# The odd layer's mixer of a decoder step as one program, with three of four channel tiles convolved on TensorE

## What is computed

```python
mod = (silu(c) @ ada_w[l] + ada_b[l])          # 6 x 1024 per layer, one row for each of 9 conditions
sh1, sc1, g1, sh2, sc2, g2 = split(mod, 6)
def odd_mixer(h, w_in, w_out, pool_w, pool_scale, conv_w, conv_b, ln_g, ln_b, pool_hist, conv_hist):
    u, a, gt = split(h @ w_in, [512, 1024])
    # causal window means of u (windows 2, 4, 8, 16, one for each 128 channels), minus u, times pool_w
    pool_out = einsum(pooled - u, pool_w) * pool_scale
    glu_ext = concatenate([conv_hist, a * sigmoid(gt)])
    cv = depthwise_conv(glu_ext, conv_w) + conv_b   # 31 taps, 512 channels
    cv = layer_norm(cv) * ln_g + ln_b               # over the 512 channels
    return concatenate([pool_out, silu(cv)]) @ w_out, u_ext[:, -15:], glu_ext[:, -30:]
```

## Time and profile before

| | us |
|---|---|
| span of the profiled execution | 3444.1 |
| time of that execution | 3445.84 |
| median of three executions | 3447.33 |
| PE busy | 3095.5 (90%) |
| DVE busy | 1291.0 (37%) |
| ACT busy | 1012.0 (29%) |
| GpSimd busy | 628.9 (18%) |
| mean granted TensorE clock | 0.939 |

### The profile page before, as it was taken

How to read it: one execution, slowest core, us unless ns; L and a number is a source line. 1 busy time by engine, 2 the same in 40 slices (tenths; PEclk the granted TensorE clock), 3 DMA queues, 4 the chain that set the end, 5 groups by cost and what they waited for, 6 DMA issues and landing times. The chain is left out here.

```text
span 3444.1 us, 45149 instructions
## 1 busy us (share of the span) xinstructions
PE 3095.5 (90%) x17877; PEld 2776.2 (81%) x17877; DVE 1291.0 (37%) x2017; ACT 1012.0 (29%) x1528; POOL 628.9 (18%) x368
## 2 busy tenths in 40 slices
PE   4799999888876988999999997979697999999997
PEld 3798899633332988999999987957397999999997
DVE  4155660366422173222222263069217222222225
ACT  3233432366432242212222132223223121222221
POOL 1211101111111212111221121162111222112210
PEclk7899999899998989999999999989698999999998
DMA  5322222100264221111111131030511111111112
GB/s 218 112 86 81 87 81 74 52 1 1 77 201 145 83 77 49 38 36 49 49 49 36 37 128 51 28 104 7 167 55 60 49 49 43 31 48 49 49 38 104
DMA packets 236584, 239.12 MB, mean 69 GB/s; under 512 B 7619, under 2 KB 194423, under 8 KB 236181
## 3 DMA queue, kind: packets, MB, share of 16 engines
q1 hardware_dynamic: 221317, 205.72, 19.0%
q0 software_dynamic: 5120, 16.78, 1.5%
q10 hardware_dynamic: 10016, 14.78, 1.2%
HBM read 207.74 MB, written 29.99 MB: 69 GB/s over the span
## 5 line engine op out<-in xcount | busy, mean ns | idle before, releaser
L614 PE MATMUL PS<-trunk_x_hi,trunk_w_hi 128*128 128x364 f32 x2208 | 740.3, 335 | 88.3 <-POOL trunk_w_lo L738 32.4
L615 PE MATMUL PS<-trunk_x_lo,trunk_w_hi 128*128 128x364 f32 x2208 | 737.3, 334 | 0.0
L616 PE MATMUL PS<-trunk_x_hi,trunk_w_lo 128*128 128x364 f32 x2208 | 735.3, 333 | 0.0
L746 POOL TENSOR_TENSOR trunk_w_lo<-trunk_w_raw,trunk_w_hi 128x1024 fp32r<-128x1024 f32 x128 | 307.0, 2398 | 1320.0 <-ACT trunk_w_hi L924 1229.7
L614 PE MATMUL PS<-hidden,trunk_w_hi 128*128 128x364 f32 x1536 | 507.9, 331 | 0.0
L615 PE MATMUL PS<-hidden,trunk_w_hi 128*128 128x364 f32 x1536 | 505.9, 329 | 0.0
L616 PE MATMUL PS<-hidden,trunk_w_lo 128*128 128x364 f32 x1536 | 505.5, 329 | 0.0
L614 PEld LDWEIGHTS PS<-trunk_x_hi,trunk_w_hi 128*128 128x128 f32 x2208 | 424.2, 192 | 90.4 <-POOL trunk_w_lo L738 33.3
L615 PEld LDWEIGHTS PS<-trunk_x_lo,trunk_w_hi 128*128 128x128 f32 x2208 | 424.5, 192 | 0.0
L616 PEld LDWEIGHTS PS<-trunk_x_hi,trunk_w_lo 128*128 128x128 f32 x2208 | 423.7, 192 | 0.0
L1175 DVE TENSOR_TENSOR M<-M,PS 128x364 f32<-128x364 f32 x336 | 178.4, 533 | 440.9 <-PE PS L616 440.9
(11 more groups left out here) (378 smaller groups left out, 3892.6 us busy)
## 6 DMA issues: line engine op xcount, KB each, us to landing
trunk_w_raw<-mlp_w SPq DMA_DIRECT2D x128, 512.0 KB
rec_ada_w<-ada_w SPq DMA_DIRECT2D x24, 1024.0 KB, 5.1
spare<-cache_sb_k SPq DMA_DIRECT2D x64, 256.0 KB, 3.2
values<-cache_sb_v POOLq DMA_DIRECT2D x64, 256.0 KB, 3.6
rec_w_raw<-even_w_in SPq DMA_DIRECT2D x28, 512.0 KB
x_scratch<-x_new ACTq DMA_DIRECT2D x9, 1456.0 KB, 5.9
x_new<-x_scratch SPq DMA_DIRECT2D x6, 1456.0 KB, 13.0
trunk_x_old<-x_scratch SPq DMA_DIRECT2D x6, 1456.0 KB, 9.9
```

The lines of the kernel that those rows point to most:

```text
L614: pe.matmul(out, hi, xh, start=first, stop=False)
L615: pe.matmul(out, hi, xl, start=False, stop=False)
L616: return pe.matmul(out, lo, xh, start=False, stop=last)
L746: pool.tensor_tensor(wl[:, u % 4, :], raw[:, u % 2, :], wh[:, u % 4, :].bitcast(F32), ALU.subtract).then_inc(s_lo, 1)
```

## The change

The eight modulation chunks leave the odd mixer. `recurrence` gets two more (14 in place of 12), so its bursts run on to the last dense tile, and the last turn, the bias sum and `coefs` stand at its end. `trunk` of layer 0 gets six: one in each of the groups 1 to 6, as four bursts of two products (behind hidden chunks 1 and 2 and down chunks 0 and 1) and a turn in down chunk 2. They use banks 6 and 7, one weight buffer of 512 KB that SP loads between the tiles of the group, and one ACT copy and one DVE addition per group. PE waits once, ahead of the loop, for DVE to clear bank 6.

The odd mixer becomes one block. Tiles 0, 1 and 2 are convolved on PE and tile 3 on DVE. For PE, SP copies each of four 32-channel strips of a tile four times, each shifted by one more column, onto the four groups of partitions of `S4` (16 copies for a tile, SBUF to SBUF, two tile buffers). A product then contracts 4 taps x 32 channels and gives 32 channels; the four strips go to four groups of 32 output partitions. 31 taps are 8 such steps; the products are plain float32, not split. Their weights `taps` are made by three GpSimd instructions from a turned table of the taps. The gate product writes straight into `G`, ACT copies u into `U`, and the squares are added on DVE in place of GpSimd.

```diff
@@ trunk: SP
-            def load_group(g):
+            def load_mod(g, b):
+                sp.wait_ge(s_am, g * 4 + (b - 3))
+                sp.dma_start(wa[:, :, :], ada_v[:, 2 * b:2 * b + 2, bass.ds(g * (4 * P) + CH0 * 4 * P, 4 * P)])\
+                  .then_inc(s_wa, 16)
+
+            def load_group(g, mod=False):
                 for u in range(8):
+                    if mod and u == 2:
+                        load_mod(g, 0)
+                    if mod and u == 6:
+                        load_mod(g, 1)
...
+                if mod:
+                    load_mod(g, 2)
+                    load_mod(g, 3)
@@ trunk: PE
+            def mod_burst(g, b):
+                pe.wait_ge(s_wa, g * 64 + 16 * (b - 3))
+                for i in range(2):
+                    k = 2 * b + i
+                    q = pe.matmul(PS[CG * (k % 4):CG * (k % 4) + SEG, 6, :], core.cT[:, k, 0:SEG], wa[:, i, :],
+                                  start=(k < 4), stop=(k >= 4), skip_group_check=True)
+                q.then_inc(s_am, 1)
...
+                if phase in (1, 2, 3, 4) and s == 7:
+                    mod_burst(g, phase - 1)
+                if phase == 5 and s == 4:
+                    mod_turn(g)
...
+            if with_mod:
+                pe.wait_ge(s_az, 1)
             with pe.Fori(1, G - 1) as g:
                 for c in range(NC3):
-                    hidden_phase(g, c)
+                    hidden_phase(g, c, False, lambda s: modulation(g, c, s))
@@ recurrence
-    CHUNKS = [(0, c) for c in range(4, 12)] + [(1, c) for c in range(4)]
+    CHUNKS = [(0, c) for c in range(4, 12)] + [(1, c) for c in range(6)]
...
+            mod_turn(NCH - 1)
...
+            mod_add(NCH - 1)
             coefs()
@@ odd_mixer: SP
+            for k in range(NPE):
+                sp.wait_ge(s_G, k + 1)
+                if k >= 2:
+                    sp.wait_ge(s_cm, k - 1)
+                else:
+                    sp.wait_ge(s_z, 1)
+                for b in range(4):
+                    for s in range(4):
+                        sp.dma_start(S4[CG * s:CG * s + CG, k % 2, b, 0:GX - s], G[CG * b:CG * b + CG, k, s:GX])\
+                          .then_inc(s_sh[k], 16)
@@ odd_mixer: PE
+            def conv(k):
+                pe.wait_ge(s_sh[k], 16 * 16)
+                pe.wait_ge(s_tp, k + 1)
+                if k == 0:
+                    pe.wait_ge(s_hl, HT)
+                    pe.wait_ge(s_tc, 1)
+                    pe.wait_ge(s_rc, 4)
+                if k >= 2:
+                    pe.wait_ge(s_cv, k - 1)
+                for g in range(NG):
+                    fl = dict(start=(g == 0), stop=(g == NG - 1), skip_group_check=True)
+                    for h in range(2):
+                        for b in range(4):
+                            pe.matmul(PS[CG * b:CG * b + CG, 2 * (k % 2) + h, :], taps[:, k, g, b, :],
+                                      S4[:, k % 2, b, 4 * g + 512 * h:4 * g + 512 * h + 512], **fl)
+                    for b in range(4):
+                        x = S4[:, k % 2, b, CHI + SEQ:].rearrange("p (s t) -> p s t", s=NSEQ)[:, :, 4 * g:4 * g + TQ]
+                        q = pe.matmul(PS[CG * b:CG * b + CG, 4 + k % 2, 0:NS].rearrange("p (s t) -> p s t", s=NSEQ),
+                                      taps[:, k, g, b, :], x, **fl)
+                q.then_inc(s_cm, 1)
...
+            for k in range(NPE):
+                conv(k)
+                if k >= 1:
+                    mean_part(k - 1)
+            mean_part(NPE - 1)
+            for k in range(NPE, HT):
+                mean_part(k)
+            mean_tails()
+            for g in range(HT):
+                pool_product(g)
+            pe.wait_ge(s_sa, HT - 1)
+            pe.wait_ge(s_po, HT)
+            column_sums(pe, core, 6, SUMS, sq[:, 0, :], True).then_inc(s_ss, 1)
+            pe.wait_ge(s_r, 1)
+            spread(pe, core, 3, r).then_inc(s_bc, 1)
@@ odd_mixer: DVE
+            k = HT - 1
...
+            with dve.Fori(1, CWID) as j:
+                w = core.convw[:, bass.ds(j * HT + k, 1)]
+                dve.wait_ge(s_acc, j + 1)
+                dve.scalar_tensor_tensor(out=cv[:, k, 0:SEQ], in0=G[:, k, bass.ds(j, SEQ)], scalar=w,
+                                         in1=cv[:, k, 0:SEQ], op0=ALU.mult, op1=ALU.add)
+                dve.scalar_tensor_tensor(out=samples(cv[:, k, :]), in0=tail(G, k)[:, :, bass.ds(j, TQ)], scalar=w,
+                                         in1=samples(cv[:, k, :]), op0=ALU.mult, op1=ALU.add).then_inc(s_acc, 1)
@@ odd_mixer: GpSimd
+            pool.wait_ge(s_tc, 1)
+            for k in range(NPE):
+                w = tap_cols.rearrange("p (g k b) -> p k g b", g=NG, k=HT)[:, k]
+                pool.tensor_tensor(taps[:, k], w.unsqueeze(3).to_broadcast([P, NG, 4, CG]),
+                                   cols(core, "fold").unsqueeze(1).unsqueeze(1).to_broadcast([P, NG, 4, CG]), ALU.mult)\
+                    .then_inc(s_tp, 1)
```

More of the change, by code:

```diff
@@ L1044, in _ @@
                 rest_of_group(g)
+                if with_mod:
+                    act.wait_ge(s_am, g * 4 + 1)
+                    act.activation(mod_rows[:, :], PS[:, 6, :], ACT.Copy).then_inc(s_ar, 1)
+            for u in range(4):
+                high_weights_of_group(G - 1, u)
+            rest_of_group(G - 1)
             u0 = 8 + 8 * G
@@ new lines, in _ @@
+            for g in range(HT):
+                act.activation(U[:, g, PH:PH + SEQ], Ut[:, g, 0:SEQ], ACT.Copy)
+                act.activation(U[:, g, PH + SEQ:].rearrange("p (s t) -> p s t", s=NSEQ)[:, :, PH:], samples(Ut[:, g, :]),
+                               ACT.Copy).then_inc(s_U, 1)
+            for k in range(NPE):
+                act.wait_ge(s_cm, k + 1)
+                b = core.vec[:, CONV_B + k:CONV_B + k + 1]
+                act.activation(cv[:, k, 0:SEQ], PS[:, 2 * (k % 2):2 * (k % 2) + 2, :].rearrange("p b c -> p (b c)"),
+                               ACT.Identity, bias=b)
+                act.activation(cv[:, k, SEQ:T], PS[:, 4 + k % 2, 0:NS], ACT.Identity, bias=b).then_inc(s_cv, 1)
@@ new lines, in _ @@
+            act.wait_ge(s_ss, 1)
+            act.activation(rt[:, :], PS[0:TB, 6, SUMS * NBK:(SUMS + 1) * NBK], ACT.Sqrt, scale=1.0 / HALF,
+                           bias=cols(core, "eps")[0:TB, :]).then_inc(s_rt, 1)
+            for k in range(HT):
+                act.wait_ge(s_y, k + 1)
+                act.activation(core.M[:, HT + k, :], cv[:, k, :], ACT.Silu, scale=core.vec[:, LN_G + k:LN_G + k + 1],
+                               bias=core.vec[:, LN_B + k:LN_B + k + 1]).then_inc(s_o, 1)
@@ new lines, in coefs @@
+            def coefs():
+                n = 0
+                for g, m_at, plus in ((1, 2, 0.0), (2, 4, 1.0), (3, 5, 0.0)):
+                    ng = core.vec[:, (4 + g) * KT:(4 + g + 1) * KT].unsqueeze(2).to_broadcast([P, KT, SEG])
+                    to = core.coef[:, 1, g].rearrange("p (k c) -> p k c", c=SEGP)[:, :, 0:SEG]
+                    mod = core.mod[:, 1, :].rearrange("p (f c) -> p f c", c=SEGP)[:, m_at * KT:(m_at + 1) * KT, 0:SEG]
+                    dve.tensor_scalar(to, mod, plus, None, ALU.add).then_inc(s_mod, 1)
+                    n += 1
+                    dve.wait_ge(s_mod, n)
+                    dve.tensor_tensor(to, to, ng, ALU.mult)
@@ L2469, in _ @@
                 dve.tensor_copy(rows[0:n, i, :], PS[0:n, 4 + i, :]).then_inc(s_rc, 1)
-            ada.finish(dve)
+            dve.memset(cv[:, :, T:TP], 0.0).then_inc(s_cz, 1)
+            coefs()
+            k = HT - 1
+            b, w0 = core.vec[:, CONV_B + k:CONV_B + k + 1], core.convw[:, k:k + 1]
+            dve.sem_inc(s_acc, 1)
+            dve.wait_ge(s_G, HT)
+            dve.tensor_scalar(cv[:, k, 0:SEQ], G[:, k, 0:SEQ], w0, b, ALU.mult, ALU.add)
+            dve.tensor_scalar(samples(cv[:, k, :]), tail(G, k)[:, :, 0:TQ], w0, b, ALU.mult, ALU.add).then_inc(s_acc, 1)
@@ new lines, in _ @@
+            dve.wait_ge(s_muc, 1)
+            for k in range(HT):
+                dve.tensor_tensor(cv[:, k, :], cv[:, k, :], mu, ALU.subtract).then_inc(s_c, 1)
+            for k in range(1, HT):
+                dve.wait_ge(s_sq, k + 1)
+                if k >= 2:
+                    dve.wait_ge(s_sa, k - 1)
+                dve.tensor_tensor(sq[:, 0, :], sq[:, 0, :], sq[:, k, :], ALU.add).then_inc(s_sa, 1)
+            dve.wait_ge(s_rt, 1)
+            dve.reciprocal(r[:, :], rt[:, :]).then_inc(s_r, 1)
```

416 lines of the change are left out of this document (170 added, 246 removed).

## The result

The changed kernel takes 3393.9 us (median of four executions, 3387.3 to 3395.8) where the kernel before, measured beside it, takes 3446.2: a ratio of 0.9844 (95% interval 0.9831 to 0.9857), 52 us less. The forecast was 3392. A later set of five executions took 3384.8, a ratio of 0.9835 (0.9820 to 0.9849), 58 us less. The profiled execution took 3394.2 us, with a span of 3392.6. In what follows PE is TensorE, DVE is VectorE, ACT is ScalarE, and SP is the engine that issues most of the DMAs; the mixer's edges are ACT's first instruction in it and ACT's first in trunk 1.

The account below looks back on a forecast made before the run. DVE's convolution was taken to bound the mixer's middle stage, and PE the loop of trunk 0. With 98.9 us removed and 44.6 added, 3445.84 becomes 3391.5; the forecast was 3392 us, range 3368 to 3424.

Parts of the forecast that it names:

- The bound: In the odd mixer's middle stage before the change: DVE's convolution sets it, busy 126.9 of 128.0 us, PE beside it.
- cover: In the new mixer's convolution: PE is through at 87 us, 21 us ahead of DVE's end at 108.5.
- Column groups side by side: In PE's new convolution: products in four column groups run side by side, so a tile takes 19.5 us.
- Shifted copies: Ahead of PE's convolution: a tile's 16 copies take 13 us at 214 GB/s, plus 2 for landing.
- DVE's start: At the new mixer's beginning: DVE's convolution starts 24 us in (22 to 29).
- DVE's taps: In DVE's one-tile convolution: waiting for the tap before adds 0.10 us, so 31 taps at 1.50 take 46.5 us.
- rival 3's first case: In DVE's tap loop: branch and wait cost 0.4 us per tap, not 0.1 (9 us); whole rival 14 in 100.
- The sign named for it: In DVE's tap loop: a pair above 1.6 us without GpSimd would say the wait was priced too low.
- GpSimd's take: Beside DVE's convolution: GpSimd's pooling takes 38 us again, as before the change (bounds 30 and 66).
- The tail: From DVE's last tap to the mixer's end: mean, squares, pooled outputs, column sums and silu, from 108.5 to 144.2 us.
- Added elsewhere: Outside the mixer: the moved modulation products add 35.3 us in trunk 0 and 9.3 in the recurrence, together 44.6.
- The sum: Over the whole kernel: 98.9 us removed in the mixer, 44.6 added elsewhere, 54.3 less.

Follow-up runs that it names:

- The longer copies: Changed kernel with each tile's 16 shifted copies made twice, the second time once the first have landed, PE waiting for both: 3397.9 us, ratio 0.9875.
- the second execution: Second profiled execution of the changed kernel, without an edit: mixer 148.1 us; its set of executions has a median of 3384.8 us.

## Why the prediction was right, point by point

- *The bound.* DVE sets the middle of the mixer in the changed kernel too: busy 78 of 86 us, with PE through 34 us ahead of its end. Right; the forecast had 20 to 21 us of cover. The longer copies showed that 27 us a tile would have used it up.
- *Column groups side by side.* Right, and shown: 1.71 us for eight products, 1.71 for two. The tile was sized at 19.5 us and takes 14.6 at the high clock, since I had taken 0.97 per four products from a lone burst (114.77 to 115.74 in the earlier trace rows); in a row they cost 0.86. The tails of 64 columns were put at 0.5 a step, a guess, and take 0.11. Left out was the low clock, which made the first tile 17.6. All of this was under cover.
- *Shifted copies.* Right: 15.5 us from the first issue at 2287.72 to the start of PE at 2303.25 (forecast 13 + 2), at 193 GB/s over the first 14 us (2288 to 2302) and 214 later (2324 to 2333). The Trainium skill's 189 ("SBUF — State Buffer", "Door 1: The DMA port swizzle") lies a little below that, and neither figure changes the sum.
- *DVE's start.* 26.1 in place of 24. Of GpSimd's pooling 4.6 us fall on the coefficient steps, which the forecast had not placed there; without it the start is at 21.6.
- *DVE's taps.* The step that failed. 0.10 for the wait was read from coefficient steps, which form no registers; in the loop, with one tile, each tap's registers stand behind the wait too. 1.73 in place of 1.50, 6.6 us over the convolution. That is rival 3's first case, 0.4 per tap and 9 us, at three quarters of its size: over the 1.40 of the two alternating tiles a tap costs 0.33 more. The sign named for it, a pair above 1.6 us without GpSimd, is there.
- *GpSimd's take.* 38 forecast, 37.4 measured by leaving it out. Of that 4.6 lie ahead of the start. So DVE's end adds up as 108.5, + 6.6 for the taps, - 2.4 for the start without pooling (21.6 against 24), - 0.7 for the pooling: 112.0.
- *The tail.* 35.7 forecast, 36.1 measured, and the sum is luck in part. ACT's copy of the mean begins 5.0 us behind the last tap, where 2.9 were forecast: the first two mean products take 3.6 us, at a granted clock of 0.50, and the rows that the price came from had 0.84 (2407.63 to 2416.57 before). The pooled outputs take 9 us in place of 7. Against that the subtractions and squares take 6 in place of 7, the column sums 2.1 in place of 3.8, and the way from the root to the last silu 11.6 in place of 12.3.
- *Added elsewhere.* 35.3 + 9.3 = 44.6 forecast, 45.4 measured in one execution and 33.3 in the other, so the closeness of the first is luck. What holds in both is the loop, where a group costs 5.54 (forecast 5.67), and the end of the recurrence, from ACT's last copy of the dense product to its first table load in the attention, which grew by 3.5 us (from 1.95 to 5.4; forecast 3.6). The last copy itself stands 3.1 and 1.2 us later than before, where the bursts and a turn were booked with 5.7: no run shows that term. The attention, which nothing touches, was 2.1 us longer in one and 6.0 shorter in the other, and trunk 0 36.7 and 34.6 longer (forecast 35.3).
- *The sum.* 95.0 saved in place of 98.9, 45.4 added in place of 44.6, and trunk 1 with what follows 1.8 us shorter (966.3 against 968.1): 51.5 us from span to span, where the forecast had 54.3. The last 1.8 are within the scatter of that stage (964.5 to 970.6 over these kernels). In the second execution the same sum is 65.4. The part that is reproduced, and by which the prediction is to be judged, is the mixer: 95.0 against 98.9. Its largest error, 6.6 us for the taps, was half made up by 3.1 in the other direction.

## What to carry to other kernels

Products with 32 stationary columns in four column groups, issued in turn, ran four at a time here, and issued group by group they did not (1.71 us for eight against 1.71 for two). That made it worth while to put all four tiles of the depthwise convolution on TensorE, with shifted copies that bring four taps into one contraction. In a hardware loop a wait for the instruction just before exposed the register instructions behind it (0.25 us per tap); let each instruction wait for one further back, or write the loop out. To price what GpSimd takes from VectorE, take GpSimd's work away, and look ahead of the loop too: small instructions there were stretched more than tenfold (2.22 and 2.89 us in place of 0.2). And compare two kernels by a distance that is reproduced: here the edges of the mixer were, within 0.1 us, and the stretches ahead of it were not, by 12.

## What was not expected of the hardware

- Register instructions of DVE's sequencer run ahead while the engine works, and cost nothing, unless a wait stands ahead of them that is met late: the gap ahead of a tap was 0.25 us then, and 0.04 to 0.06 without the loop or without the late wait.
- A coefficient step of 72 columns took 2.89 us beside GpSimd in place of 0.23, and a 64-column tap 2.96 in place of 0.28. The step that took 2.22 us, from 2298.88, stood beside one GpSimd instruction of the same length (2.22 us from 2298.83).
- After 8 us of idle time PE took 3.6 and 3.0 us for the first two steps and 1.83 from the third on; the granted clock was 0.50, 0.61 and 1.00 in them. Of two products each, the third pair of the pooling took 3.75 us in the tail after 4.75 us of idle time, at 0.50, and 1.94 at 1.00 where the work stood closer together.
